# Expert selection on one engine, in single steps, in a hybrid diffusion backbone (one core)

## What is computed

```python
def peer_ffn(h, ...):   # cut; 8 heads, 128 x 128 experts of one neuron each, top 16 per head
    q = (h @ wq) -> two halves per head              # 2 x 128 scores per head and token
    s1, i1 = top_k(q1 @ keys1.T, 16)
    s2, i2 = top_k(q2 @ keys2.T, 16)
    s, pos = top_k(s1[:, None] + s2[None, :], 16)    # over the 16 x 16 sums
    expert = i1[pos // 16] * 128 + i2[pos % 16]
    gate = softmax(s)
    y = sum over the 8 x 16 chosen of gate * gelu(u[expert] . h) * v[expert]
```

## Time and profile before

| | |
|---|---|
| median of three runs | 5212.61 us (5211.89 to 5221.45) |
| the profiled execution | 5207.43 us, span 5205.8 us |
| mean granted clock of TensorE in it | 0.951 |
| TensorE, matmuls | 4671.4 us busy, 90% |
| VectorE | 3231.9 us, 62% |
| GpSimd | 1963.4 us, 38% |
| ScalarE | 1637.0 us, 31% |

### The profile page before, as it was taken

One profiled execution on the slowest core, in us unless ns is written; L12 is line 12 of the kernel. 1 busy time (PEld: TensorE's weight loads), 2 busy tenths in 40 slices (PEclk: granted clock), 3 DMA queues, 4 the chain that ended last, 5 costly groups with the idle time before them and its releaser, 6 DMA issues.

```text
span 5205.8 us, 78220 instructions
## 1 busy us (share of the span) xinstructions
PE 4671.4 (90%) x26310; PEld 3910.4 (75%) x26310; DVE 3231.9 (62%) x6217; ACT 1637.0 (31%) x3053; POOL 1963.4 (38%) x1948
## 2 busy tenths in 40 slices
PE   8888889999898886999998987789999987999997
PEld 6558778989888885665655664588788986888886
DVE  2663553757568976266566746636475755677777
ACT  2221441443433338000000023324144447233232
POOL 1110120000057876377777511103010116676652
PEclk9888999999999999999999997799999999999999
DMA  4221113555549991699999932111355561899997
GB/s 153 97 105 49 37 35 130 173 195 183 189 151 356 338 364 50 245 383 371 375 373 382 406 145 76 70 55 41 128 183 183 187 196 46 322 366 351 351 375 265
DMA packets 316684, 1103.49 MB, mean 212 GB/s; under 512 B 59392, under 2 KB 108672, under 8 KB 267872
## 3 DMA queue, kind: packets, MB, share of 16 engines
q1 hardware_dynamic: 165024, 648.09, 35.3%
q0 software_dynamic: 151488, 453.35, 23.6%
HBM read 1037.13 MB, written 62.03 MB: 211 GB/s over the span
## 4 chain that ended last, share of the span: by engine, by line
PE 60%; POOL 12%; DVE 10%; issue 8%; DMA 5%; ACT 3%; POOLq 1%; ACTq 0%; DVEq 0%; PEldq 0%; SPq 0%
PE PS L1231 14%; PE PS L1296 12%; PE PS L1320 7%; POOL arena L656 7%; PE PS L1190 5%; DMA arena<-in_experts,arena 5%; POOL arena L662 4%; PE PS L1305 4%; PE PS L907 3%; PE PS L905 3%; PE PS L1152 3%; DVE PS L2377 2%; PE PS L984 2%; PE PS L963 1%; PE PS L1041 1%
## 5 line engine op out<-in xcount | busy, mean ns | idle before, releaser
L1231 PE MATMUL PS<-hS,wS 128*128 128x256 f32 x9216 | 1164.9, 290 | 111.1 <-DVE wS L2402 78.0
L1231 PEld LDWEIGHTS PS<-hS,wS 128*128 128x128 f32 x9216 | 1149.1, 198 | 126.3 <-DVE wS L2402 89.0
L2377 DVE SCALAR_TENSOR_TENSOR PS<-arena,PS 128x1024 f32<-128x1024 f32 x762 | 979.0, 1285 | 336.0 <-DMA arena<-in_experts,arena 312.9
L656 POOL DMA_INDIRECT arena<-hx,arena x768 | 849.0, 1105 | 396.4 <-issue 229.3
L662 POOL DMA_INDIRECT arena<-in_experts,arena x768 | 770.9, 1004 | 513.7 <-DVE PS L2377 295.1
L1296 PE MATMUL PS<-hS,ring 128*128 128x256 f32 x4096 | 927.2, 379 | 3.1 <-POOLq L392 3.1
L1296 PEld LDWEIGHTS PS<-hS,ring 128*128 128x128 f32 x4096 | 778.6, 190 | 167.0 <-issue 60.5
L2402 DVE TENSOR_TENSOR wS<-ring,wS 128x1024 fp32r<-128x1024 f32 x384 | 469.6, 1224 | 323.8 <-ACT wS L1609 322.7
L1305 PE MATMUL PS<-ring,arena 128*128 128x512 f32 x1024 | 473.5, 606 | 46.0 <-DVE arena L2521 45.9
L1715 ACT ACTIVATE arena<-PS 128x256 f32<-128x256 f32 x256 | 98.7, 385 | 1192.9 <-PE PS L1296 1186.3
L1609 ACT ACTIVATE wS<-ring 128x1024 fp32r<-128x1024 f32 x384 | 403.7, 1053 | 8.1 <-DMA ring<-in_experts 5.1
(11 more groups left out here) (316 smaller groups left out, 5851.3 us busy)
## 6 DMA issues: line engine op xcount, KB each, us to landing
ring<-in_experts SPq DMA_DIRECT2D x256, 1024.0 KB
ring<-in_experts SPq DMA_DIRECT2D x384, 512.0 KB
ring<-in_wcat SPq DMA_DIRECT2D x80, 1024.0 KB
hx<-arena SPq DMA_DIRECT2D x384, 128.0 KB
ring<-in_wq SPq DMA_DIRECT2D x40, 1024.0 KB
arena<-in_rpb POOLq DMA_DIRECT2D x96, 128.0 KB, 2.6
arena<-hx,arena POOLq DMA_INDIRECT x768, 6.3
arena<-in_experts,arena POOLq DMA_INDIRECT x768, 7.7
```

Source lines behind the costliest of these rows:

```text
L656: pool.indirect_dma_start(out=aX[n][:, k:k + 1], out_offset=None, in_=src, in_offset=bass.IndirectOffsetOnAxis(ap=at[:, k:k + 1], axis=0)) ...
L1231: mm = pe.matmul(bank[6 + c % 2][:, 0:PASS], u[:, k, :], hS[:, h, k, :], start=(part == 0 and k == 0), stop=(part == 2 and k == KD - 1))
L2377: op = dve.scalar_tensor_tensor(out=total, in0=row, scalar=aX[n][:, k:k + 1], in1=total, op0=ALU.mult, op1=ALU.add)
```

## The change

The selection is done by VectorE alone. `products`, its two semaphores and its places in GpSimd's queue go. `positions` works on all eight heads at once and runs after the last head, so nothing of it stands among the first five heads any more. A new generator, `lookups`, makes one step of each one-hot (eight of 1024 elements per partition), of each product (eight) and of each sum (eight), in that order. All of this stands ahead of `yield pause`, so that only the softmax's normalisation follows it. `some_steps` takes the rate as an argument, and the counter is capped at one more than the rate; the own selection's rate becomes 1.25, the others stay at 1.0 and 0.6. The diff, without the hunks that drop names only and with `positions` cut to its first operations, which all lose their slice of heads:

```diff
--- before.py
+++ after.py
@@ -635,19 +634,6 @@
-                def products(hf):
-
-                    ps_ = t.get("pass", 0)
-                    full = [P, HALF, TOPK, TOPK]
-                    pool.wait_ge(s["eq_want"], 2 * ps_ + hf + 1)
-                    for tb in range(2):
-                        tfh = tifs[tb].rearrange("p (h o) k -> p h o k", o=2)[:, HALF * hf:HALF * (hf + 1)]
-                        for v in ((0, 1) if hf == 0 else (1,)):
-                            eq = eqs[hf][tb][v]
-                            last = pool.tensor_tensor(eq, eq, tfh[:, :, v, :].unsqueeze(2).broadcast_to(full), ALU.mult)
-                    last.then_inc(s["eq_done"], 1)
-                    t["pass"] = ps_ + hf
-
@@ -671,8 +657,7 @@
                 load_pass(f0 + 2)
-                products(0)
-                products(1)
+                t["pass"] = t.get("pass", 0) + 1
@@ -686,8 +671,7 @@
                     if not second:
-                        products(0)
-                        products(1)
+                        t["pass"] += 1
@@ -696,14 +680,11 @@
                         for n in range(16):
-                            if n == 13:
-                                products(0)
                             pool.wait_ge(s["pq_done"], 16 * t["pass"] + n + 1)
                             take_activations(3, f0, range(32 + 2 * n, 34 + 2 * n))
                         pool.wait_ge(s["s_done"], 8 * (t["pass"] + 1))
+                        t["pass"] += 1
                         for r in range(P):
-                            if r == SECOND_HALF:
-                                products(1)
@@ -1926,72 +1907,79 @@
-            def positions(hf, count):
-
-                hs, hps = slice(HALF * hf, HALF * (hf + 1)), slice(2 * HALF * hf, 2 * HALF * (hf + 1))
+            def positions():
+
                 for tb in range(2):
-                    dve.tensor_copy(tifs[tb][:, hps], tius[tb][:, hps])
-                    dve.tensor_copy(pbfs[tb][:, hs], pus[tb][:, hs])
-                    dve.tensor_single_scalar(pas[tb][0][:, hs], pus[tb][:, hs], 3, ALU.logical_shift_right)
-                    last = dve.tensor_single_scalar(pas[tb][1][:, hs], pus[tb][:, hs], 2, ALU.logical_shift_right)
+                    dve.tensor_copy(tifs[tb], tius[tb])
+                    dve.tensor_copy(pbfs[tb], pus[tb])
+                    dve.tensor_single_scalar(pas[tb][0], pus[tb], 3, ALU.logical_shift_right)
+                    last = dve.tensor_single_scalar(pas[tb][1], pus[tb], 2, ALU.logical_shift_right)
                 link(last)
                 yield 0
...
-                full = [P, HALF, TOPK, TOPK]
-                for tb in range(2):
-                    yield 0
-                    for v, at in ((0, pafs[tb]), (1, pbfs[tb])):
-                        last = dve.tensor_tensor(eqs[hf][tb][v], at[:, hs].unsqueeze(3).broadcast_to(full),
-                                                 iota[:, 0:TOPK].unsqueeze(1).unsqueeze(1).broadcast_to(full), ALU.is_equal)
-                last.then_inc(s["eq_want"], 1)
-                dve.wait_ge(s["eq_want"], count)
+                yield 0
 
             def by_head(tb, v):
                 return sels[tb][:, v, :].rearrange("p (h k) -> p h k", k=TOPK)
 
-            def look_up(hf, tb, v):
-
-                return dve.tensor_reduce(by_head(tb, v)[:, HALF * hf:HALF * (hf + 1)], eqs[hf][tb][v], AX, ALU.add)
+            def lookups():
+
+                full = [P, HALF, TOPK, TOPK]
+                each = [(hf, tb, v) for hf in range(2) for tb in range(2) for v in range(2)]
+                for hf, tb, v in each:
+                    at = (pafs, pbfs)[v][tb][:, HALF * hf:HALF * (hf + 1)]
+                    last = dve.tensor_tensor(eqs[hf][tb][v], at.unsqueeze(3).broadcast_to(full),
+                                             iota[:, 0:TOPK].unsqueeze(1).unsqueeze(1).broadcast_to(full), ALU.is_equal)
+                    if (hf, tb, v) == each[-1]:
+                        link(last)
+                    yield 0
+                for hf, tb, v in each:
+                    tfh = tifs[tb].rearrange("p (h o) k -> p h o k", o=2)[:, HALF * hf:HALF * (hf + 1), v, :]
+                    last = dve.tensor_tensor(eqs[hf][tb][v], eqs[hf][tb][v], tfh.unsqueeze(2).broadcast_to(full), ALU.mult)
+                    if (hf, tb, v) == each[-1]:
+                        link(last)
+                    yield 0
+                for hf, tb, v in each:
+                    dve.tensor_reduce(by_head(tb, v)[:, HALF * hf:HALF * (hf + 1)], eqs[hf][tb][v], AX, ALU.add)
+                    yield 0
 
             def retrieve(ps_, stored, pause):
 
                 for h in range(HEADS):
                     yield from head_lists(h, 8 * ps_ + h + 1)
-                    if h == HALF - 1:
-                        yield from positions(0, 2 * ps_ + 1)
                     if h == HALF:
                         yield -1
 
@@ -2004,13 +1992,8 @@
                                       ).then_inc(s["gexp"], 1)
                 dve.wait_ge(s["gexp"], 2 * ps_ + 2)
                 yield 0
-                yield from positions(1, 2 * ps_ + 2)
-                yield 0
-                for tb in range(2):
-                    tfh = tifs[tb].rearrange("p (h o) k -> p h o k", o=2)[:, HALF:]
-                    last = dve.tensor_tensor(eqs[1][tb][0], eqs[1][tb][0],
-                                             tfh[:, :, 0, :].unsqueeze(2).broadcast_to([P, HALF, TOPK, TOPK]), ALU.mult)
-                link(last)
+                yield from positions()
+                yield from lookups()
 
                 yield pause
                 dve.wait_ge(s["gready"], 2 * ps_ + 2)
@@ -2023,18 +2006,8 @@
                     last = dve.reciprocal(gsums[tb], gsums[tb])
                 link(last)
                 for tb in range(2):
-                    dve.tensor_tensor(by_head(tb, 2), bss[tb], gsums[tb].unsqueeze(2).broadcast_to(wide), ALU.mult)
-
-                dve.wait_ge(s["eq_done"], 2 * ps_ + 1)
-                for tb in range(2):
-                    for hf, v in ((1, 0), (0, 0), (0, 1)):
-                        yield 0
-                        look_up(hf, tb, v)
-
-                dve.wait_ge(s["eq_done"], 2 * ps_ + 2)
-                for tb in range(2):
-                    yield 0
-                    look_up(1, tb, 1).then_inc(s["sel_ready"], 1)
+                    dve.tensor_tensor(by_head(tb, 2), bss[tb], gsums[tb].unsqueeze(2).broadcast_to(wide), ALU.mult
+                                      ).then_inc(s["sel_ready"], 1)
 
@@ -2402,9 +2375,9 @@
                         dve.tensor_tensor(wS[:, 2 * (c % 2) + 1, :], ring[:, c % SLOTS, 0:D], wS[:, 2 * (c % 2), :].bitcast(F32),
                                           ALU.subtract).then_inc(s["slot_free"], 1)
 
-                    def some_steps(steps, c):
-
-                        taken["steps"] += 0.6 if second else 1.0
+                    def some_steps(steps, c, rate):
+
+                        taken["steps"] = min(taken["steps"] + rate, 1 + rate)
                         while taken["steps"] >= 1 and taken["from"] <= c:
                             taken["steps"] -= 1
                             taken["from"] = next(steps, 0)
@@ -2425,7 +2398,7 @@
                             pass
                         for c in range(norm_at):
                             low_gathered(c)
-                            some_steps(own, c)
+                            some_steps(own, c, 1.25)
                         for _ in own:
                             pass
                         t["pass"] += 1
@@ -2449,7 +2422,7 @@
                         pass
                     for c in range(meet, PK):
                         low_gathered(c)
-                        some_steps(steps, c)
+                        some_steps(steps, c, 0.6 if second else 1.0)
                         while second and taken["rows"] < min(P, (c - meet - 1) * P // (PK - 4 - meet)):
                             early_row()
                     for _ in steps:
```

More of the change, by code:

```diff
@@ L1949, in positions @@
                 for tb in range(2):
-                    last = dve.tensor_tensor(pa3[tb][:, hs], pa3[tb][:, hs], pa2[tb][:, hs], ALU.max)
+                    last = dve.tensor_tensor(pa3[tb], pa3[tb], pa2[tb], ALU.max)
                 link(last)
                 for tb in range(2):
-                    last = dve.tensor_tensor(pafs[tb][:, hs], pafs[tb][:, hs], pa3[tb][:, hs], ALU.max)
+                    last = dve.tensor_tensor(pafs[tb], pafs[tb], pa3[tb], ALU.max)
                 link(last)
@@ L1967, in positions @@
                 for tb in range(2):
[L1968 removed]
+                    last = dve.tensor_tensor(pa3[tb], pa3[tb], pa2[tb], ALU.min)
                 link(last)
                 for tb in range(2):
[L1971 removed]
+                    last = dve.tensor_tensor(pbfs[tb], pbfs[tb], pa3[tb], ALU.subtract)
                 link(last)
[L1973 removed]
```

25 lines of the change are left out of this document (11 added, 14 removed).

## The result

| | before | after |
|---|---|---|
| median of four runs each, us | 5217.03 (5211.89 to 5222.63) | 5172.47 (5163.48 to 5179.57) |
| the profiled execution, us | 5207.43 | 5179.57 |
| its span, us | 5205.8 | 5177.9 |
| TensorE's mean granted clock in it | 0.951 | 0.953 |
| ratio of the times | | 0.9913, 95% interval 0.9894 to 0.9933 |

The change makes the kernel 44.6 us faster; the forecast was 5171 in a range of 5150 to 5192. A few executions are slow, at a lower granted clock; the ratios leave them out and the medians don't, except for own_rate_1, where one of ten took 6094.29 us at a granted clock of 0.734.

The account below looks back on a forecast made before the run. TensorE bounds passes (0,0) and (1,2), with holes at each selection's end; GpSimd's queue paces (0,2). Savings of 39.4 us there plus 2.5 in (0,2) make 41.9, taken from 5212.6: 5171 us, range 5150 to 5192.

Parts of the forecast that it names:

- first selection, (0,0): Pass (0,0), chunks 28 to 47: of 9.4 us lost, 2.8 stay for ScalarE's table loads and loop, 6.6 saved.
- first selection, (1,2): Pass (1,2), first selection: same code and load as in (0,0), so 6.6 us saved again.
- second selection, (0,0): Pass (0,0), second selection's 68 chunks: 15.85 us over in the last 35, less what stays, 13.7 us saved.
- second selection, (1,2): Pass (1,2), second selection: the same saving as in (0,0), put at 12.5 us.
- price: nothing while that slack holds: Beside the chunks of (0,0) and (1,2): VectorE's added steps cost nothing; without slack, 5 us over some ten chunks.
- What takes their place: New generator in (0,0) and (1,2): 57 steps against 43, 1.14 us a big step, products 1.217, nothing saved up.
- Pass (0,2): GpSimd's queue sets the pace: 9.5 us gained without its products, 7 lost to held-up issues, net gain 2.5 us.
- Rival 1: VectorE becomes the bound in pass (0,2), its 9 us more lengthen the pass; 5182 us, chance 0.18.
- Rival 2: Pass (0,2) runs evenly, 70 chunks at 3.33 us each, 18 us gained there; 5155 us, chance 0.15.
- Rival 3: Double steps meet ScalarE's table loads, TensorE waits for both, half of the 39.4 us remains; 5190 us, chance 0.10.
- Rival 4: VectorE's product takes 3.39 us by itself, without GpSimd's part, so the kernel is slower; 5249 us, chance 0.03.
- Rival 5: The change does nothing, as the sums still pile up behind the softmax; about 5211 us, chance 0.02.

Follow-up runs that it names:

- own_rate_1: The changed kernel with the first selection at 1.0 and not 1.25 steps a chunk; 5197.55 us in the median of nine runs, ratio 0.9971 to before.
- early_half: The changed kernel with the first half's positions, one-hots and products moved back ahead of the `-1`, on VectorE, first rate 1.1875; 5167.72 us, ratio 0.9895 to before.
- own_rate_13: The changed kernel with the first selection at 1.3125 and not 1.25 steps a chunk; 5460.72 us on a slower chip, ratio 0.9879 to before.
- cap_only: The kernel before with the step counter capped at one more than the rate, nothing else; 5198.78 us, ratio 0.9965 to before.
- gp_free: The kernel before with GpSimd's products moved to VectorE, two to a step, and no cap; 5185.56 us, ratio 0.9945 to before.
- after_third: The changed kernel, unedited, run again on another, slower chip; 5460.32 us against 5525.68 for before there, ratio 0.9899.

## Why the prediction held, and where its terms were off

**What bounds the kernel and the stalls that go.** Held. The terms against the stages, chunks and the query stage behind them counted together:

| term | predicted, us | after, us |
|---|---|---|
| first selection, (0,0) | 6.6 | 5.6 |
| first selection, (1,2) | 6.6 | 4.5 |
| second selection, (0,0) | 13.7 | 15.2 |
| second selection, (1,2) | 12.5 | 12.6 |
| sum | 39.4 | 38.0 |

The time came out within 1.5 us of the forecast, and part of that is luck: the kernel before measured 5217.0 with a fourth run and not 5212.6, the gain is 44.6 us and not 41.9, and of the terms the 39.4 us of the two passes are seen (37.3 and 38.0) while the 2.5 of (0,2) are not.

The first selections were set too high. The step that failed is "price: nothing while that slack holds", for the last steps at chunk 43. VectorE's timeline there:

```profile
1079.97 1.21 DVE L2375 TENSOR_TENSOR wS<-ring,wS 128x1024 fp32r<-128x1024 f32 x1
1081.10 1.21 DVE L1976 TENSOR_REDUCE arena<-arena 128x64 f32<-128x1024 f32 x1
1082.23 0.47 DVE L2002 TENSOR_REDUCE arena<-arena 128x8 f32<-128x128 f32 x2
...
1083.57 0.49 DVE L2320 SCALAR_TENSOR_TENSOR arena<-arena 128x128 f32<-128x128 f32 x2
...
1085.30 1.22 DVE L2375 TENSOR_TENSOR wS<-ring,wS 128x1024 fp32r<-128x1024 f32 x1
```

The prediction had 1.3 us of steps and 1.8 of index work here. It is 4.2 us between two splits: a sum (1.13), the softmax's last operations (1.3) and the index work (1.7). That the last of the eight sums falls in the same gap was left out. Of the 2.1 us of room, the split ahead had 1.8 left, and this one comes 2.45 late. So TensorE waits 0.67 us in (0,0) and 0.77 in (1,2); with the sum elsewhere (early_half, own_rate_13) the wait is gone. That is 0.7 of the 1.0 missing in (0,0), and 0.8 of 2.1 in (1,2); the rest is of the size by which this stage varies with the clock (185.7 to 187.8 us over the six profiles whose first selection is after's). Over these six the mean saving in the chunks is 4.4 us, so the term was indeed too high, by about 2. Pass (1,2) with its 17.2 us stays below the 19 to 21 that the prediction named as its sign.

The second selection of (0,0) was set too low. The prediction carried 0.05 us a chunk over 2.88 through all 68 chunks, 3.9 us with the softmax's 0.4. (Its "1.75" is the 35 chunks alone; its 13.7 counts the 0.4 too, and by the same sum its 12.5 would be 12.4.) The 41 chunks ahead of the softmax do take 2.92 each (984 matmuls in 119.82 us), but the 27 behind it 2.89 (78.02 us), and 2.4 us are left over in all.

**What takes their place.** Held: 1.217 us a product; steps of 1.13 to 1.14 us; no split of a second selection is late, and the counter saves nothing up. The prediction did not divide its gain between the cap and the release of GpSimd; they are worth 17 and 21 us.

**Pass (0,2).** The gain's one visible term held. GpSimd's timeline at the end of the query stage, for the earlier trace rows:

```profile
1537.92 0.95 POOL L642 DMA_INDIRECT arena<-hx,arena  x1 [0.30 <-issue]
1539.17 0.94 POOL L648 DMA_INDIRECT arena<-in_experts,arena  x1 [0.31 <-issue]
```

The first row is taken 69.8 us after the pass's query products begin (1469.4), where before it was 74.2 (1485.2, then 1559.35 in the earlier trace rows): 4.4 us earlier, 4.5 predicted. The net could not be resolved. The pass is 2.3 us longer in the profile of after (530.2 against 527.8), and its rows part is 401.7 in the mean of three profiles after the change, 400.9 in the mean of before and the two kernels built on it (400.0, 405.4, 397.4): +0.8, give or take some 5, where -2.5 was predicted. With the gain of 9.5 that puts the loss near 10 and not 7, the upper end of the 5 to 11 given. No profile shows (0,2) as the source of any of the 45 us.

**The rivals.** Rival 1, VectorE bound in (0,2) and 9 us longer: not seen at that size; of the 13 us that the lookups cost there, 10.5 are longer issues, which leaves its mechanism some 3. Rival 2, (0,2) evenly at 3.33 us a chunk and 18 us shorter: falls, the rows part did not shrink. Rival 3, stall handed on: falls in the second selections (0.37 us), and is the 0.7 us at chunk 43 in the first; own_rate_1 shows what it would have been with thirteen steps left over, 12 us a pass. Rival 4: falls, in two kernels. Rival 5, sums still in a piece: falls, but cap_only shows that the cap, without the new order, was enough to break the piece up. The new order without the cap was not run.

**What stays open.** The medians gained 44.6 and 48.1 us in two sets of runs, the two passes 38.0 and 37.3 in the profiles. The start and (0,2) vary by 6 to 8 us from profile to profile with the same code, and before's profiled execution was 10 us under its median. So the 7 to 11 us between are not placed with certainty. gp_free has the same gap, 31.5 by the medians and 21 in the stages. The table has a hint: the span without the five stages is 3934 us for before and 3933 to 3947 for the other nine, 3939.5 in the mean. Before's one profile was thus some 5 us short outside the stages that the change touches, and that would be about half of the gap.

## What to carry to other kernels

A stall at the end of a side job need not be that job's work: here half came from a step counter that kept saving up while the job was told to wait, and half from a helper engine that made the same instruction take 3.39 us and not 1.217. Moving the helper's work onto the loaded engine was then cheaper than sharing it, and the duration of one instruction in the two settings said so before the change. Count what is left over when the steps run out: at 1.25 steps a chunk it costs 0.7 us, at 1.0 it costs 12. The room for a late operation is read where nothing is late (2.1 us here); an existing hole, by its lateness less the wait it causes, shows only what the operation ahead of it had left (0.9 to 1.8). And where a stage takes one of two times in the same code, read the clock of the stretch behind each wait first: 1.5 us here hid a price of 0.7.

## What the runs showed of the hardware

Two chips ran the same code 6% apart. In the gathered passes, the difference lies where transfers are heavy. Here is the stretch 1540 to 1930 us, for after and then after_third (busy of PE, PEld, DVE, ACT, POOL; clock, DMA, GB/s):

```profile
1540.00:1930.00 390.00, 340.46 (x2621) 330.08 (x2622) 339.77 (x466) 151.50 (x223) 311.06 (x256) 0.96 0.98 352
```

```profile
1540.00:1930.00 390.00, 313.58 (x2179) 297.16 (x2178) 285.00 (x461) 124.56 (x187) 254.31 (x222) 0.89 0.85 289
```

The rows of (0,2) take 449 to 482 us there over the three kernels, where after's take 404, with 289 GB/s and not 352 in after_third, while the first stages of (0,0) and (1,2), 185.5 to 187.6 us, and the second one of (1,2), 198.0 to 198.3, are what they were. Whether slower transfers are the cause or go with another one isn't shown. The change's ratio is the same on both chips, 0.99, though its gain lies in stages that this difference doesn't touch: 56 us by the ratio there, with an interval from 33 to 79, which holds the 45 to 48 of the first chip. A profile's absolute times in a stage with heavy transfers hold for the chip that they were taken on.
